# The first mixer of a two-block network on one core: latent attention placed beside the recurrence's levels, its roots kept as columns by token

## The reference, cut to what matters

```python
u = rmsnorm(h, mix_norm[layer])
z = jnp.einsum('bld,de->ble', u, w_in[e])
hq, hf, hi, hg, cq, ckv, kr = jnp.split(z, IN_SPLITS, axis=-1)
o_a = hgrn2_mixer(hq, hf, hi, hg, lower_bounds[e], hgrn_out_norm[e])   # gated recurrence
o_b = mla_mixer(cq, ckv, kr, ...)                                      # latent attention
mix = jnp.einsum('ble,ed->bld', jnp.concatenate([o_a, o_b], axis=-1), w_out[e])

def mla_mixer(...):
    q = rmsnorm(cq, qa_g) @ w_q_up          # 4 heads of 128 + 64
    k_nope, v = split(rmsnorm(ckv, kva_g) @ w_kv_up)
    q = rope_tail(rmsnorm(q, qn_g), cos, sin)
    k = rope_tail(rmsnorm(concat(k_nope, kr), kn_g), cos, sin)
    o = softmax(where(mask, q k^T * scale, -inf)) v
```

## Time and profile before

| what | value |
|---|---|
| median of three runs | 1329.74 us (1326.45 to 1330.06) |
| the profiled execution: its own time | 1330.67 us |
| its span, first to last instruction | 1328.8 us |
| PE busy | 1284.4 us, 97% of the span |
| DVE busy | 910.2 us, 68% |
| ACT busy | 738.1 us, 56% |
| mean granted clock of PE | 0.98 of full speed |

### The profile page before, as it was taken

One profiled execution on the slowest core, in us unless ns is written; L12 is line 12 of the kernel. 1 busy time (PEld: TensorE's weight loads), 2 busy tenths in 40 slices (PEclk: granted clock), 3 DMA queues, 4 the chain that ended last, 5 costly groups with the idle time before them and its releaser, 6 DMA issues.

```text
span 1328.8 us, 24830 instructions
## 1 busy us (share of the span) xinstructions
PE 1284.4 (97%) x10389; PEld 1254.0 (94%) x10389; DVE 910.2 (68%) x1550; ACT 738.1 (56%) x1255; POOL 6.3 (0%) x15
## 2 busy tenths in 40 slices
PE   5998999999999999999999999999999999999997
PEld 5897778999999999999999999999999989999997
DVE  4579636666544587544586699974787857999655
ACT  5745223655444576533555566664666766666544
POOL 1000000000000000000000000000000000000000
PEclk9999969999999999999999999999989999999998
DMA  7232104455555265555366365566255334665630
GB/s 256 82 120 83 61 0 127 130 188 175 184 172 169 81 223 190 186 182 188 122 220 190 102 209 191 183 209 199 79 174 191 128 111 137 198 192 193 203 127 32
DMA packets 58891, 205.54 MB, mean 155 GB/s; under 512 B 6515, under 2 KB 8860, under 8 KB 58524
## 3 DMA queue, kind: packets, MB, share of 16 engines
q1 hardware_dynamic: 57104, 201.77, 46.9%
q10 hardware_dynamic: 1676, 2.19, 0.5%
HBM read 202.87 MB, written 1.06 MB: 153 GB/s over the span
## 4 chain that ended last, share of the span: by engine, by line
PE 86%; DVE 7%; ACT 5%; issue 1%; DMA 0%; ACTq 0%; DVEq 0%
PE PS L361 68%; PE PS L409 7%; PE PS L443 2%; DVE WL L346 1%; PE PS L392 1%; ACT WH L339 1%; PE PS L372 1%; PE PS L2149 1%; PE PS L490 1%; PE PS L676 1%; ACT EE L2307 1%; PE PS L713 0%; ACT L502 0%; PE PS L714 0%; PE PS L808 0%
## 5 line engine op out<-in xcount | busy, mean ns | idle before, releaser
L346 DVE TENSOR_TENSOR WL<-RAW,WH 128x1024 fp32r<-128x1024 f32 (+2 forms) x385 | 460.7, 1202 | 232.1 <-ACT WH L339 231.5
L339 ACT ACTIVATE WH<-RAW 128x1024 fp32r<-128x1024 f32 (+2 forms) x385 | 391.9, 1038 | 243.1 <-PE PS L361 215.4
L361 PE MATMUL PS<-UH,WH 128*128 128x256 f32 (+2 forms) x1576 | 448.7, 285 | 6.4 <-DVE WL L346 2.7
L361 PE MATMUL PS<-UH,WL 128*128 128x256 f32 (+2 forms) x1576 | 448.5, 285 | 0.0
L361 PE MATMUL PS<-UL,WH 128*128 128x256 f32 (+2 forms) x1576 | 448.2, 284 | 0.0
L361 PEld LDWEIGHTS PS<-UH,WH 128*128 128x128 f32 (+1 forms) x1576 | 299.2, 190 | 7.2 <-DVE WL L346 3.0
L361 PEld LDWEIGHTS PS<-UH,WL 128*128 128x128 f32 (+1 forms) x1576 | 299.3, 190 | 0.0
L361 PEld LDWEIGHTS PS<-UL,WH 128*128 128x128 f32 (+1 forms) x1576 | 297.8, 189 | 0.0
L361 PE MATMUL PS<-HL,WH 128*128 128x272 f32 (+1 forms) x512 | 145.8, 285 | 0.0
L361 PE MATMUL PS<-HH,WH 128*128 128x272 f32 (+1 forms) x512 | 145.7, 285 | 0.0
L361 PE MATMUL PS<-HH,WL 128*128 128x272 f32 (+1 forms) x512 | 145.4, 284 | 0.0
(11 more groups left out here) (381 smaller groups left out, 1988.4 us busy)
## 6 DMA issues: line engine op xcount, KB each, us to landing
RAW<-wpack SPq DMA_DIRECT2D x363, 512.0 KB, 3.8
RAW<-wpack SPq DMA_DIRECT2D x16, 384.0 KB, 3.6
RAW<-wpack SPq DMA_DIRECT2D x6, 256.0 KB, 3.1
X<-xin SPq DMA_DIRECT2D x1, 1088.0 KB, 5.1
C<-cst SPq DMA_DIRECT2D x1, 1072.0 KB, 10.1
HB<-bias_rows ACTq DMA_DIRECT2D x1, 1024.0 KB, 5.2
out<-X SPq DMA_DIRECT2D x4, 256.0 KB, 2.3
VF<-cst ACTq DMA_DIRECT2D x1, 512.0 KB, 4.0
```

The source lines that it names most:

```text
L339: a.e.activation(WH[n % NH][:, 0:w], RAW[n % NR][:, 0:w], ACT.Copy).then_inc(*a.mark("wh", n))
L346: v.e.tensor_tensor(WL[n % NH][:, 0:w], RAW[n % NR][:, 0:w], WH[n % NH][:, 0:w].bitcast(f32), ALU.subtract).then_inc(*v.mark("wl", n))
L361: ins = t.e.matmul(o, part(n, hw, kw, a, b), x(kx), start=first and not i and not p, stop=last and i == len(kcs) - 1 and p == 2)
```

## The change

It does five things, all in the first mixer.

- **Order.** The `hi` units come after the units of the latent attention. PE projects `hf`, `hq`, `cq` and half of `ckv` before the diagonal product. `kr`, the latent sums, `qup`, `kvup` and `value_up` stand between levels 0 and 3; `hi` and the heads' sums stand around level 4. All four calls of `keep_going` in the mixer go (106 products); those elsewhere stay. ACT and DVE split the weights at fixed places of their lists, `act_split(a, n)` and `dve_split(v, n)`. DVE reaches unit 24 by line `dve_split(v, 25)`; units 25 and on (`wout`) are split by the loop at the mixer's end.
- **Roots as columns.** The sums of squares of the latents and of the heads are made with the tokens on partitions: 128 tokens of squares are the stationary operand and one column of ones moves. A sum is a column, its root and reciprocal are taken over 6 or 12 elements a partition. Queries are no longer divided by their root or the latent's: that factor and the scale go into the softmax's exponential, by row. The keys' root is spread over the features with an identity product. The latents are not divided by the token's root (`r2` corrects the sums).
- **Fewer, wider evictions.** The four heads of a rise are one group of four banks with one mark; ACT evicts the queries, DVE the keys. The copies of the transposed keys `KT` move from DVE to ACT.
- **Mask with maximum.** Two of the three score tiles use one `tensor_tensor_reduce` a head in place of an addition over all heads and a reduction.
- **Front tile.** The first root also sums 128 tokens for the front tile instead of 16. POOL clears two more pieces of memory.

The evictions of `hf`, `hq` and `hg` and the arithmetic of the gates stay; `KT`, `hg` and the `chunk`s keep their work and change places. The diff, cut to what the prediction speaks of:

```diff
-    rows("hi", "w_in", 0, 1024, 1536)
...
+    rows("hi", "w_in", 0, 1024, 1536)
...
+        def in_front(st):
+            return 128 if st == "m" else NM
...
-        RQ, SQB, OUTA, QE, KD, PB = ACC[1], LF, K, Q, K, B
+        LSQ, KSQ, KRSQ, QSQ, QRSQ = CQ, CQ, ACC[1][0:64, 1, :], LF, RT
+        R2, L2, GK = CO[:, 0:3], CO[:, 10:13], CO[:, 13:14]
+        LAT = CO[:, 4:10].rearrange("p (x i) -> p x i", x=2)
+        QSC, KSC = (CO[:, a:a + 12].rearrange("p (i h) -> p i h", h=4) for a in (16, 28))
...
             def latent_sums():
+                b = banks.take(t, ("lat",), ("lm",))
                 for x in range(2):
-                    t.wait_ge("cqsq", x)
-                    b = banks.take(t, ("rq", x), ("rqs", x))
                     for m in range(2):
-                        ins = t.e.matmul(PS[:, b, 0:T], ONE[:, :], SQB[:, 2 * x + m, :], start=m == 0, stop=m == 1)
-                    ins.then_inc(*t.mark("mix", "rq", x))
-
-            def query_up(hs):
-                for h in hs:
-                    n = unit_at["qup", h // 4]
-                    m = 128 if h < 4 else 64
-                    a = m * (h % 4)
-                    b = banks.take(t, ("qup", h), ("qn", h))
-                    products(t, PS[0:m, b, 0:T], n, [(0, 0), (1, 1)], a, a + m, lambda k: CH[:, k, :],
-                             lambda k: CL[:, k, :], lambda k: ("cl", k)).then_inc(*t.mark("mix", "qup", h))
-
-            def key_up():
-                n = unit_at["kvup", 0]
+                        t.wait_ge("lsq", 2 * x + m)
+                    for i, a in enumerate(WIDE):
+                        for m in range(2):
+                            ins = t.e.matmul(PS[:, b, 3 * x + i:3 * x + i + 1], LSQ[:, 2 * x + m, a:a + 128],
+                                             ONE[:, 0:1], start=m == 0, stop=m == 1)
+                ins.then_inc(*t.mark("mix", "lat"))
+            def head_sums_by_token(key, sq, rsq, freed):
+                t.wait_ge("zero", 8)
+                t.wait_ge("hsq", key, 0)
+                t.wait_ge("hsq", key, 1)
+                b = banks.take(t, ("hs", key), freed)
+                for i, a in enumerate(WIDE):
+                    for hh in range(4):
+                        o = PS[:, b, 4 * i + hh:4 * i + hh + 1]
+                        t.e.matmul(o, sq(hh)[:, a:a + 128], ONE[:, 0:1], start=True, stop=False)
+                        ins = t.e.matmul(o, rsq(hh)[:, a:a + 128], ONE[:, 0:1], start=False, stop=True)
+                ins.then_inc(*t.mark("mix", "hs", key))
+            def up(key, x, ks, m, freed):
+                n = unit_at[key, x]
+                b = banks.take(t, (key, x), freed, 4)
...
+            def spread_columns(key, col, freed, heads):
+                t.wait_ge("hrec", key)
+                b = banks.take(t, ("hr", key), freed, heads)
+                for hh in range(heads):
+                    for i, (a, z) in enumerate(TILES):
+                        ins = t.e.matmul(PS[:, b + hh, a:z], col(i, hh, z - a).to_broadcast([z - a, 128]),
+                                         ID[0:z - a, 0:z - a], start=True, stop=True)
+                ins.then_inc(*t.mark("mix", "hr", key))
...
-            project("hf", 0, "ev")
-            project("hf", 1, "ev")
-            project("hq", 0, "ev")
-            project("hq", 1, "ev")
-            values(0)
-            keep_going(t, 30)
+            project("hf", range(4), "ev")
+            project("hq", range(4), "ev")
+            project("cq", range(2), "cl0")
+            project("ckv", (0,), "cl1")
             t.wait_ge("kd", 3)
             t.wait_ge("qsilu", 3)
             intra(0, K, Q)
+            project("ckv", (1,), "cl1")
+            level(0)
+            project("kr", (0,), "ev")
+            latent_sums()
+            level(1)
+            up("qup", 0, [(0, 0), (1, 1)], 128, ("qn",))
+            up("qup", 1, [(0, 0), (1, 1)], 64, ("gr", "q"))
+            level(2)
+            up("kvup", 0, [(0, 2), (1, 3)], 128, ("kn",))
+            spread_columns("l", lambda i, hh, n: LAT[0:n, 1, i:i + 1], ("rkv",), 1)
+            value_up()
+            level(3)
+            values(0)
+            head_sums_by_token("q", lambda hh: QSQ[:, hh, :], lambda hh: TMA[:, hh, :], ("qm",))
+            level(4)
             values(1)
-            level(0)
-            project("cq", 0, "ev")
-            level(1)
-            project("ckv", 0, "ev")
-            keep_going(t, 26)
-            level(2)
-            project("kr", 0, "ev")
-            level(3)
-            latent_sums()
-            query_up(range(0, 4))
-            sig.also(("used", unit_at["qup", 0]), ("mix", "qup", 3))
-            level(4)
-            query_up(range(4, 8))
-            sig.also(("used", unit_at["qup", 1]), ("mix", "qup", 7))
-            key_up()
+            head_sums_by_token("k", lambda hh: KSQ[:, hh, :], lambda hh: ACC[1][:, 1, :], ("hroot", "k"))
             level(5)
-            columns(1, RQ[:, 1, :], ("rqr", 1))
-            value_up()
+            rotate("q", QR, 4)
+            project("hg", range(2), "ev")
+            rotate("k", KR, 1)
+            spread_columns("k", lambda i, hh, n: KSC[0:n, i, hh:hh + 1], ("rope", "k"), 4)
...
...
+            def queries():
+                b0, b1 = banks.at["qup", 0], banks.at["qup", 1]
+                a.wait_ge("mix", "qup", 0)
+                a.e.activation(QN[:, :, :], PS[:, b0:b0 + 4, 0:T], ACT.Copy).then_inc(*a.mark("qn"))
+                a.wait_ge("scan")
+                a.wait_ge("qn")
+                a.e.activation(QSQ[:, :, :], QN[:, :, :], ACT.Square).then_inc(*a.mark("hsq", "q", 0))
+                a.wait_ge("mix", "qup", 1)
+                a.e.activation(QRSQ[:, :, :], PS[0:64, b1:b1 + 4, 0:T], ACT.Square).then_inc(*a.mark("hsq", "q", 1))
...
+                a.wait_ge("mix", "kt", i)
+                a.e.activation(KT[0:z - p0, i, :], PS[0:z - p0, banks.at["kt", i], :], ACT.Copy).then_inc(*a.mark("kt", i))
+            act_split(a, 27)
...
-                    ins = a.e.activation(P[:, hh, :], P[:, hh, :], ACT.Exp, bias=STT[0:m, i, hh:hh + 1], scale=sc2,
+                    ins = a.e.activation(P[:, hh, :], P[:, hh, :], ACT.Exp, bias=STT[0:m, i, hh:hh + 1],
+                                         scale=QSC[0:m, i, hh:hh + 1],
                                          accum_out=STT[0:m, i, 4 + hh:5 + hh])
...
+            def latent_roots():
+                v.wait_ge("hroot", "l")
+                v.e.reciprocal(LAT[:, :, :], LAT[:, :, :]).then_inc(*v.mark("lr", 0))
+                v.wait_ge("lr", 0)
+                v.e.tensor_tensor(LAT[:, :, :], LAT[:, :, :], both(rooted("m", 0, 128, 3)), ALU.mult).then_inc(
+                    *v.mark("hrec", "l"))
+                v.wait_ge("hrec", "l")
+                v.e.tensor_tensor(L2, LAT[:, 0, :], LAT[:, 0, :], ALU.mult).then_inc(*v.mark("lr", 1))
...
+            def query_rest():
+                b = banks.at["qup", 1]
+                v.wait_ge("hsq", "q", 1)
+                v.e.tensor_scalar(QR[:, :, :], PS[0:64, b:b + 4, 0:T], g("qr", 0, 64), None, ALU.mult).then_inc(
+                    *v.mark("gr", "q"))
...
+            prepare(0)
             attention(0)
-            prepare(0)
-            dve_split(v, unit_at["hi", 2] + NH)
+            latent(0, 0)
+            latent(0, 1)
+            dve_split(v, 13)
             attention(1)
             prepare(1)
-            latent(0)
+            latent(1, 0)
+            latent(1, 1)
+            key_rest()
+            dve_split(v, 14)
+            latent_means()
+            dve_split(v, 15)
             attention(2)
             prepare(2)
-            latent(1)
+            latent_roots()
+            dve_split(v, 17)
+            query_rest()
             attention(3)
             prepare(3)
-            dve_split(v, unit_at["kr", 0] + NH)
-            v.wait_ge("mix", "kr", 0)
-            v.e.tensor_tensor(KR[:, 0, :], PS[0:64, banks.at["kr", 0], 0:T], R[0:64, :], ALU.mult).then_inc(
-                *v.mark("ev", "kr", 0))
+            keys()
+            v.wait_ge("krsq")
+            v.e.tensor_scalar(KR[:, 0, :], KR[:, 0, :], g("krn", 0, 64), None, ALU.mult).then_inc(*v.mark("gr", "k"))
+            dve_split(v, 19)
+            query_means()
             attention(4)
             prepare(4)
-            for x in range(2):
-                v.wait_ge("rqs", x)
-                v.e.reciprocal(RQ[:, x, :], RQ[:, x, :]).then_inc(*v.mark("rqr", x))
-            dve_split(v, unit_at["qup", 0] + NH)
-            query_up(range(0, 4))
+            dve_split(v, 21)
+            query_roots()
             attention(5)
             prepare(5)
-            query_up(range(4, 8))
-            dve_split(v, unit_at["kvup", 0] + NH)
-            for h in range(4):
-                v.wait_ge("mix", "kup", h)
-                v.wait_ge("rqr", 1)
-                v.e.tensor_tensor(KN[:, h, :], PS[:, banks.at["kup", h], 0:T], RQ[:, 1, :], ALU.mult).then_inc(
```

(73 more changed lines are left out.)

295 lines of the change are left out of this document (145 added, 150 removed).

## The result

The changed kernel takes 1337.0 us (median of 17 runs, 1330.3 to 1339.7) where the kernel before takes 1329.7 (17 runs beside it, 1326.5 to 1332.4): a ratio of 1.0049, 95% interval 1.0035 to 1.0064. It is slower by 0.5%, a little more than the 0.3% that a measurement tells from nothing. The forecast was 1330; the time is inside the range and within half a microsecond of the rival "slower: the clock in the one-column stretches", 1336.5. The profiled execution took 1339.7 us, the longest of the 17; its span is 1337.9, against 1330.67 and 1328.8 before. What it shows of the clock is therefore the large end of what the kernel does; the table of all runs further down gives the middle.

What follows compares the result with a forecast made beforehand. PE and DVE were both taken as close to the bound, with waits between them deciding. Scores start 4.7 us earlier, +1.8 after them and +3.2 for the clock: net +0.3 on 1330.67, forecast 1330 us, range 1318 to 1338.

Steps and rivals of the forecast that it cites:

- slower: the clock in the one-column stretches: Rival: PE falls to 1.2 GHz in one-column sums and at `hg`'s wait, three more spells, +6.6, 1336.5 us; chance 0.22.
- the case that it called likeliest: The forecast itself: 1330 us, no measurable change, own range 1326 to 1334; chance 0.42.
- the main step: Up to the scores: they start at 158 to 164 us; wrong if before 155 or with more than two spells.
- The 106 products without use, -14.0: PE up to the scores: four groups of products without use go, 14.0 us less.
- The exchange on PE, +4.6: PE up to the scores: one-column sums and spreading roots replace former sums, +4.6 us, between +3 and +6.
- The four waits, +13.8: PE waits at `kr` 4.4, queries' second rise and `kvup` 2.2, level 4 4.8, `hg`'s third unit 2.4: 13.8 us.
- the second rise: PE waits 1.8 us for the queries' second rise, whose four banks overlap the first's, which ACT frees.
- The front tile, +0.2: Before the first root: the wider sum adds four instructions' worth of width, 0.2 us exposed.
- After the scores, +1.8: First tile's banks freed later, +0.2, and first `wout` split later, +1.6; together +1.8 us, between 0 and +3.
- The clock, +1.7 and +3.2: PE: two cold spells behind stalls for one, +1.7 us; slow one-column instructions and a spell behind, +3.2 us.
- four spells of 3.4: Upper bound on the clock's cost from the one-column products; the lower bound was 0, and one spell was taken.

Runs made afterwards that it cites:

- e7: Kernel before without its 106 products without use in the mixer; 1331.3 us, ratio 1.0019 against the kernel before.
- e1: Changed kernel with VectorE's queries' means moved behind level 4's attention and operands; 1327.3 us, ratio 0.9991 against the kernel before.
- e2: Changed kernel with VectorE's first half of `ckv` moved ahead of attention(1), freeing `kr`'s bank earlier; 1329.3 us, ratio 0.9991 against the kernel before.
- e10: e6 with the split of unit 25's low half moved ahead of `normed` on VectorE; 1308.9 us, ratio 0.985 against the kernel before.
- e4: Changed kernel with 38 products without use added between the queries' sums and level 4; 1334.8 us, ratio 1.0036 against the kernel before.
- e5: Changed kernel with the first two `wout` units split while VectorE waits for the recurrence's output; 1333.3 us, ratio 1.0032 against the kernel before.
- e8: Changed kernel with mask addition and maximum as two separate instructions again; 1335.7 us, ratio 1.0045 against the kernel before.
- e9: Changed kernel with the edits of e1, e2 and e5, one-column sums left in one piece; 1321.0 us, ratio 0.9923 against the kernel before.
- e3: Changed kernel with the heads' one-column products placed eight at a time behind each token tile's values' products; 1330.1 us, ratio 0.9999 against the kernel before.
- e6: Changed kernel with the edits of e1, e2, e3 and e5 together; 1314.5 us, ratio 0.9891 against the kernel before.

## Why the prediction was right, and where not

The number stands (1330 for 1337, range 1318 to 1338), the case that it called likeliest does not: what happened is the slower rival. By its own signs it is wrong in the main step: scores start at 175.4 us and not between 158 and 164, and six spells show before them, not two. That the time is still inside the range, and the rival's 1336.5 so close, is partly luck. The rival has 11.5 us of clock more than before, 16.0 were measured up to the scores, and what came after the scores was 3.2 us better than forecast for a reason that the prediction does not have. By its own steps:

- **The 106 products without use, -14.0.** Right as a part of the sum (PE's work is 8.4 us less, which is -14.0 and +5.7). e7 shows that the term has no worth of its own: taken out of the kernel before alone they give nothing.
- **The exchange on PE, +4.6.** Measured +5.7 (123.0 for 117.3). One-column instructions take 0.11 us each, 5.3 us for 48 in the queries' sums, where 4.9 was taken from rows with 0.10; the lower figure that the prediction took from the Trainium skill's page "TensorE: Matmul & The Clock Gate", section "Wait — 56ns, not 53.3ns?", was further off.
- **The four waits, +13.8.** Measured 12.9 in all, each at its place and, but for the second rise, with its releaser. This is the part that held best; e1, e2 and e10 took away the three long ones.
- **The front tile, +0.2.** Measured +0.9: the first weight product starts at 20.66 us for 19.73. The last eight of the root's sums have 128 tokens for 16 and take 0.99 us for four where they took 0.26, in series ahead of the first root.
- **After the scores, +1.8.** Its two terms are in the waits: 1.7 for 1.4 at the first tile's banks, 2.9 for 1.2 at the output projection; with 0.4 before the recurrence's output PE is idle 2.5 us more. Yet the whole was -1.4. Neither the list of the change nor the sum has what else is new here: `scores` now issues the products with `KN` of all four heads and then the four with `CQ`, where the kernel before alternates them (the rows below, first before, then after, both at 2.4 GHz). One product took 0.65 us and takes 0.51. Over all score products that is 6.7 us of work for 9.0, so -2.3; the order of these products was not tried by itself. The clock took 0.8 us less up to the output projection, and behind its start another 0.8 is gone, most of it idle time; why was not traced.

```profile
167.30 0.72 PE L714 MATMUL PS<-CQ,QR 64*128 64x272 f32 x2
167.95 0.73 PE L713 MATMUL PS<-KN,QN 128*128 128x272 f32 x2
...
175.40 2.10 PE L740 MATMUL PS<-KN,QN 128*128 128x272 f32 x8
177.43 2.10 PE L742 MATMUL PS<-CQ,QR 64*128 64x272 f32 x8
```

- **The clock, +1.7 and +3.2. This is the step that failed.** The mechanism was named and sized as one spell more behind a stall and one behind the one-column products, 4.9 us together; measured are 16.0 us more than before ahead of the scores (18.9 for 2.9). The prediction made each spell 3.4 us long, after the earlier trace rows. In the trace they are longer: the queries' sums, the stall before level 4 and level 4 itself give 10.2 us, the keys' sums with level 5, the queries' rotation and the first 5 us of `hg` 17.1. Where the clock fell in the middle of a block of sums, it stayed low through the narrow products behind it and into the wide ones. This is what the earlier trace rows had shown from 172 to 197 us; the row was quoted as evidence, and the bound "four spells of 3.4" did not use its length.

The cause is tested from both sides, and the traces at hand allow one more comparison. Seven kernels have both heads' sums in one piece. For each block of 48 one-column instructions: how long after its start the clock fell, and how long 1.2 GHz then lasted.

| trace | queries' sums: fall, spell (us) | keys' sums: fall, spell (us) |
|---|---|---|
| changed kernel | 5.3, 10.2, then a stall of 4.8 | 2.7, 17.1 |
| e1 | 5.3, 3.4 | 5.2, 3.4 |
| e2 | 2.1, 17.1, a stall of 4.8 in it | 3.2, 17.1 |
| e4 | 2.5, 10.2, filled | 5.0, 3.4 |
| e5 | 2.5, 13.6, a stall of 4.8 in it | 5.2, 3.4 |
| e8 | 5.3, 10.2, then a stall of 4.8 | 2.8, 17.1 |
| e9 | 2.9, 10.2 | 3.0, 17.1 |

The clock falls in or right at the end of all fourteen blocks, with wide products and no idle time ahead of them. In the six blocks made a part at a time (e3, e6, e10) it fell in none; e3's fall at 115.1 us comes with the stall ahead of level 4. So the sums alone are enough. So is a stall: the one of 3.3 us in the earlier trace rows, and in the changed kernel the one of 4.2 ahead of `kr`, during which the clock falls (65.8 us), have no one-column products ahead of them. The table also says what a block costs. Where the clock fell only at its end and no stall followed, it was back 3.4 us later; where it fell in the first 3.2 us, 10 to 17 us went by. Which of the two happens differs with nothing edited (e5 and e8 against the changed kernel, at the keys' sums), and what decides it stays open. The latents' 24 instructions are such a block too: in e2, e6, e9 and e10, where no stall precedes them, 3.4 to 6.8 us at 1.2 GHz begin in them or within 0.7 us behind them. In e1, where they follow right on a spell behind the stall ahead of `kr`, none does. No run breaks them up.

One trace of each kernel doesn't give the average, but every run's record has its span and mean clock. Span x (1 - clock) is half of the time at 1.2 GHz, idle time at that clock included; span x clock is the rest. Medians over the runs:

| us | half of the time at 1.2 GHz | the rest |
|---|---|---|
| kernel before (three sets of runs) | 24 to 25 | 1303 |
| changed kernel | 40 | 1295 |
| e1, level 4's wait gone | 33 | 1292 |
| e2, `kr`'s wait gone | 37 | 1292 |
| e3, sums among the values | 33 | 1296 |
| e4, level 4 filled | 36 | 1297 |
| e5, `wout` split earlier | 38 | 1294 |
| e7, before without fills | 35 | 1295 |
| e8, mask apart | 41 | 1293 |
| e9, no stalls, sums in one piece | 32 | 1288 |
| e6, no stalls, sums among the values | 25 | 1288 |
| e10, e6 with a split moved | 20 | 1287 |

The change as such won 8 us, and the clock took 15. e3 against the changed kernel, and e6 against e9, differ in the clock alone, by 7 us each: that is what the one-column blocks cost. e1 gets 7 us back from the clock and 3 from the wait. Within one kernel the rest hardly moves from run to run (e9: 1286.6 to 1289.8 where the times lie 15.6 us apart); the scatter is the clock's.

Where did the expected gain go? In the two profiled executions, up to the scores, PE's useful work fell by 8 us (14.0 removed, 5.7 added), idle time rose by 2 (12.9 for 11.0), and the clock took 16. With the waits and the order mended, it is 19 to 21 us less than before (e10: 1308.9 beside 1328.2; 1329.7 over all runs).

## What to carry to other kernels

In this kernel all fourteen blocks of 48 one-column instructions in a row took TensorE to 1.2 GHz although it had not been idle, and what came behind then ran at half speed too. Put such products a few at a time among wide ones, which here cost nothing and gave 7 us (e3). When fills are removed, list first the waits that they covered and expect more time at 1.2 GHz (e7), then look at what each consumer in the other engine's list stands behind; here three moved calls of VectorE, which cost no work at all, turned +7 us into -7 (e9), the order of the products made it -15 (e6), and a fourth moved call -19 to -21 (e10). And price a fall of the clock by the longest slow stretch that the trace shows behind small products, not by the shortest. And before a difference between two traces is called an edit's, look at a trace whose edit lies elsewhere (e5): here the same code had 3.4 and 17.1 us at 1.2 GHz.

## What was not expected of the hardware

- The clock fell from 2.4 to 1.2 GHz 2 to 5 us into every block of 48 one-column instructions, with PE 100% busy (e9: 102.97 and 105.8, 123.37 and 126.3; e1: 107.2 and 112.4, 124.4 and 129.4). In the prediction's reading of the section "What's actually happening" of the Trainium skill's page "TensorE: Matmul & The Clock Gate" they would have held it; the trace says they don't.
- A wait's price was above its length: 4.8 us gave 8 to 10 (e1). For 1.7 us at the output projection e5 measured 2.3 to 3.7, which its intervals don't tell from 1.7. For 4.2 us at `kr`, e2 gave 5.5 at the scores; for 2.4 us, e10 gave 3.7 there against e6 (150.44 for 154.14), 1.6 of it from the shorter spells.
- The combined addition and maximum runs as one instruction of 0.44 us and an accumulator read of 0.08 for each head, one head every 0.36 us, in all 1.5 us for the 2.6 of the two wide instructions (e8).
- Two kinds of score products, alternating, took 0.65 us each, and 0.51 each when four of a kind came in a row (before: 167.30 to 168.61 us; changed kernel: 175.40 to 177.43).
